# One transformer layer on eight cores: channel-major data, Q beside K and V, and one attention stream that carries the other work as fillers

## What is computed

```python
# 1. half-step SwiGLU FFN (hidden width 2816) on latents and context
x   = x   + 0.5 * g1  * swiglu(modulate(rmsnorm(x)))
ctx = ctx + 0.5 * cg1 * swiglu(modulate(rmsnorm(ctx)))
# 2. token mixer on one normalised input
h, hc = modulate(rmsnorm(x)), modulate(rmsnorm(ctx))
q, k, v, f, ga, gf = split(h @ w_in)     # 8 q heads, 2 kv heads of 128, f: 4 groups of 128
k_c, v_c = split(hc @ w_in[:, kv columns])
q, k = rope(headnorm(q)), rope(headnorm(k));  k_c = headnorm(k_c)
y_attn = softmax(q [k_c, k]^T / sqrt(128)) [v_c, v]            # 2304 keys
y_four = real(fft2(f over (2048 positions, 128 channels)))     # per group, unitary
mix = (sigmoid(ga) * (y_attn @ w_ab) + sigmoid(gf) * (y_four @ w_fb)) @ w_o
x = x + g2 * mix
# 3. second half-step SwiGLU FFN on the latents
x = x + 0.5 * g3 * swiglu(modulate(rmsnorm(x)))
```

## Time and profile before

| what | value |
|---|---|
| median of 3 runs | 2266.95 us |
| span of the profiled execution, slowest core (core 5) | 2253.1 us |
| what the median has above that span | 13.85 us |
| PE busy | 1989.8 us (88%) |
| DVE, ACT, POOL busy | 960.2, 793.6, 322.9 us |
| start, before the first FFN matmul | 0 to 65.9 us |
| first FFN | 65.9 to 690 us |
| K, V, F | 690 to 820 us |
| sequence transform | 820 to 897 us |
| input and Q of tile 0 | 897 to 942.5 us |
| attention, merge and Q, output projection | 942.5 to 1733.5 us |
| last FFN and stores | 1733.5 to 2253.1 us |

### The profile page before, as it was taken

The page is one execution under the profiler, slowest core; times in us unless marked ns, Lnnn a source line. Parts: engine busy times, 40 slices in busy tenths (PEclk is TensorE's granted clock), DMA queues, the critical chain, the costliest instruction groups (busy, mean ns, idle before and its releaser), DMA issues.

```text
span 2253.1 us, 29761 instructions; the slowest of 8 cores (2246.0 to 2253.1 us)
## 1 busy us (share of the span) xinstructions
PE 1989.8 (88%) x9570; PEld 875.1 (39%) x9570; DVE 960.2 (43%) x1310; ACT 793.6 (35%) x1338; POOL 322.9 (14%) x404
## 2 busy tenths in 40 slices
PE   2599998999997777689989998999997999899998
PEld 1244443444443333233433443343332443344344
DVE  0245345343444311554464455444533534533434
ACT  1342110111114630476758557666723310011011
POOL 1341000000004410310320121030014300000000
PEclk9899999999998898799999999999998999999999
DMA  9834244132303443400830380083046132203013
GB/s 176 174 66 75 36 77 66 32 62 38 57 14 63 75 87 101 71 1 1 141 66 1 66 141 1 1 136 66 1 84 103 30 57 38 46 2 56 1 38 112
DMA packets 46084, 138.48 MB, mean 61 GB/s; under 512 B 5104, under 2 KB 5360, under 8 KB 45808
## 3 DMA queue, kind: packets, MB, share of 16 engines
q0 software_dynamic: 31104, 109.07, 29.0%
q1 hardware_dynamic: 12528, 23.34, 3.2%
q10 hardware_dynamic: 2304, 4.20, 0.6%
HBM read 237.24 MB, written 8.39 MB: 109 GB/s over the span
## 4 chain that ended last, share of the span: by engine, by line
PE 74%; DVE 9%; issue 5%; ACT 4%; DMA 3%; POOL 3%; DVEq 0%; ACTq 0%; SPq 0%; POOLq 0%
PE ps L618 14%; PE ps L612 14%; PE ps L640 10%; PE ps L911 9%; DVE xT L645 5%; PE ps L963 5%; PE ps L946 5%; PE ps L964 4%; POOL arena L463 2%; PE ps L1052 2%; PE ps L929 2%; PE ps L444 2%; DMA tmpf<-x 2%; DVE tmpf L1001 1%; PE ps L967 1%
## 5 line engine op out<-in xcount | busy, mean ns | idle before, releaser
L626 ACT ACTIVATE tmpf<-ps 128x512 f32<-128x512 f32 (+1 forms) x198 | 113.4, 573 | 809.5 <-PE ps L612 798.9
L628 DVE TENSOR_TENSOR arena<-ps,tmpf 128x512 bf16<-128x512 f32 (+1 forms) x198 | 130.4, 661 | 494.2 <-PE ps L618 428.8
L645 DVE SCALAR_TENSOR_TENSOR xT<-ps,cols,xT 128x512 f32<-128x512 f32 x384 | 285.4, 750 | 104.4 <-PE ps L640 82.8
L640 PE MATMUL ps<-arena,ring 128*128 128x512 bf16 (+1 forms) x1168 | 278.6, 364 | 28.3 <-DVE xT L645 8.9
L612 PE MATMUL ps<-arena,ring 128*128 128x512 bf16 (+1 forms) x1136 | 258.4, 371 | 10.8 <-POOL arena L463 9.4
L618 PE MATMUL ps<-arena,ring 128*128 128x512 bf16 (+1 forms) x1072 | 242.6, 369 | 0.0
L953 ACT ACTIVATE arena<-ps 128x512 bf16<-128x512 f32 x320 | 185.5, 596 | 109.6 <-PE ps L946 102.0
L463 POOL TENSOR_SCALAR arena<-tmpf,cols 128x512 bf16<-128x512 f32 (+1 forms) x144 | 160.9, 1129 | 214.8 <-DVE tmpf L456 214.8
L911 PE MATMUL ps<-arena,ring 128*128 128x512 bf16 x768 | 171.4, 380 | 5.4 <-DVE arena L1003 5.4
L640 PEld LDWEIGHTS ps<-arena,ring 128*128 128x128 bf16 x1168 | 95.1, 96 | 189.2 <-issue 125.1
L953 ACT ACTIVATE pt<-ps 128x512 bf16<-128x512 f32 x256 | 152.4, 596 | 31.3 <-DVE tmpf L972 15.6
(11 more groups left out here) (115 smaller groups left out, 2214.1 us busy)
## 6 DMA issues: line engine op xcount, KB each, us to landing
ring<-w_in POOLq DMA_DIRECT2D x66, 512.0 KB, 8.3
ring<-w_ffn_in POOLq DMA_DIRECT2D x31, 512.0 KB, 7.2
ring<-w_ada POOLq DMA_DIRECT2D x24, 512.0 KB, 17.3
ring<-w_ffn_out POOLq DMA_DIRECT2D x16, 512.0 KB, 10.1
ring<-w_ab POOLq DMA_DIRECT2D x16, 512.0 KB, 9.4
ring<-w_o POOLq DMA_DIRECT2D x16, 512.0 KB, 9.2
out<-tmpf SPq DMA_DIRECT2D x32, 256.0 KB, 2.0
arena<-w_ffn_in POOLq DMA_DIRECT2D x13, 512.0 KB, 9.5
```

The costliest lines, as they stand in the source:

```text
L626: P.op("act", lambda e, pg=pg, sg=sg: e.activation(out=tmpf[:, sg, 0:n], in_=ps[pg][:, 0:n], func=AF.Silu), reads=[ps_b[pg]], writes=[tmpf ...
L628: P.op("dve", lambda e, pu=pu, sg=sg, jj=jj: e.tensor_tensor(out=act[par][:, jj, 0:n], in0=ps[pu][:, 0:n], in1=tmpf[:, sg, 0:n], op=ALU.mult),
L640: ins = e.matmul(ps[po][:, 0:n], wo3[:, jj % 2, m * 128:(m + 1) * 128], act[par][:, jj, 0:n], start=(jj == 0), stop=(jj == cg - 1))
L645: P.op("dve", lambda e, m=m, po=po: e.scalar_tensor_tensor(out=b["xsl"](m), in0=ps[po][:, 0:n], scalar=cols[:, b["ig"], m:m + 1], in1=b["x ...
```

## The change

The whole program behind the buffers is reordered. What it does, part by part:

- **Data layout.** x, the context and the output are laid out by the host in chunks of channels, so the PE transposes, their copies and the identity go. x is loaded by `load_x` straight into `xT`, block by block in the order latent 0, context, latent 1, 2, 3; the load of a later block waits on SP until PE has reached the block before it. The cosine and sine tables come with the last block. POOL no longer waits for ada tile 7 before it requests FFN weights; SP does before the context load.
- **Start** (`first_block`). The statistics of block 0 and the products with x are made before the ada tiles are consumed. Then the modulation is split: ACT 2 chunks, POOL 1, DVE 5.
- **Normalised input.** Elsewhere the modulation alternates between ACT and POOL.
- **FFN.** The 8 output chunks of a block are spread between the input matmuls of the next block (`carry`, `Spread`), over groups and into the K/V/Q stretch. In the last group the mixer's normalised inputs of blocks 0, context and 1 are side work.
- **K, V, F and Q in one pass** (`p1_run`). Each latent block has 10 heads (2 K, 8 Q) in a pipeline of three stages (`pipe_step`), with V and F units between them. The squares for blocks 2 and 3 are on POOL. The normalised input of each block is stored to HBM, and so is Q of blocks 0 to 2; block 3 is attended first (`ORDER2`). No barriers are left; `inherit` hands the old readers of a region to the new buffers.
- **Sequence transform** (`fourier_thunks`). It folds position n with 2048 - n and frequency m with 2048 - m: 64 half-width channel matmuls as before, then 16 sequence matmuls for each of 4 groups and some small ones. It runs as fillers in attention tile 0. ACT and DVE combine the sums, POOL writes the four quarters.
- **Attention** is one stream of 4 x 8 x 18 = 576 steps without seams, with one filler of two matmuls per step. Of the sums over keys only 3 of 18 stay on PE; 9 exponentials per head are added on DVE (8 adds and a join) and 6 on POOL (5 adds). 8 buffers hold exponentials, before 4.
- **Merge and output** (`merge_thunks`) of a tile are the 144 fillers of the next tile. Sigmoid is computed as (1 + tanh(x/2)) with the factor 0.5 in the column of the output gate. The order of the mid matmuls is ga, gf, fb, ab, in two PSUM banks. The last tile's merge runs alone, with the statistics of the first two blocks of the last FFN.
- **Stores** go from `xT` directly.

```diff
+        def first_block():
+            ...
+            for th in ffn_mh_thunks(blocks, 0)[:12]:
+                th()
+            for m in range(NCH):
+                P.op("dve", lambda e, m=m: e.tensor_tensor(out=xr[m], in0=b["xsl"](m), in1=tmpf[:, 1, :], op=ALU.mult), ...)
+            for t in range(8):
+                ada_consume(t)
+            ...
+        def load_next(bi):
+            if bi < 5:
+                P.wait("sp", [("pe", P.cnt["pe"])])
+                load_x(ORDER1[bi])
...
+                    sp = Spread(side, max(1, 2 * cg - max(1, cg // 2)))
+                    so = Spread(carry, 2 * cg)
+                    def between(sp=sp, so=so):
+                        so.pop()
+                        sp.pop()
+                    for jj in range(cg):
+                        ffn_in_unit(b, pa, jj, between)
...
+            def norm():
+                P.op("pe", lambda e: e.matmul(ps[3][:, 0:n], ones_bf, sq, start=True, stop=True), ...)
+                P.op("act", ... AF.Ln ...)
+                P.op("act", ... AF.Exp, scale=-0.5 ...)
+                P.op("dve", lambda e: e.scalar_tensor_tensor(out=o, in0=ps[pb][:, 0:n], scalar=vecs[:, vgain:vgain + 1], in1=rv, ...))
+            def cosm():
+                P.op("pool", lambda e: e.tensor_tensor(out=qc, in0=qn, in1=cos_bf[...], op=ALU.mult), ...)
+            def rope():
+                P.op("pe", lambda e: e.matmul(ps[6][:, 0:n], rperm_bf, qn, start=True, stop=True), ...)
+                P.op("dve", lambda e: e.tensor_tensor(out=rs, in0=ps[6][:, 0:n], in1=sin_bf[...], op=ALU.mult), ...)
+                P.op("dve", lambda e: e.tensor_tensor(out=dst, in0=qc, in1=rs, op=ALU.add), ...)
...
+            return mh_thunks(..., hb, 7, sqs=sq_pt, ts=(5, 5, 6, 7), sq_eng="pool")
...
+                chunks(6, wget(hga), c0, lambda k: hh[:, k, :], hh_b, 8, lambda sa=sa: late.append(lambda: tanh(6, sa)))
+                chunks(7, wget(hgf), c0, lambda k: hh[:, k, :], hh_b, 8, lambda sf=sf: late.append(lambda: tanh(7, sf)))
+                chunks(6, wget(hfb), c0, lambda k: yfour[:, k, t * 512:(t + 1) * 512], [...], 4, lambda sf=sf: gate(6, sf))
+                chunks(7, wget(hab), c0, lambda k: Y[:, k, :], Y_b, 8, fin_ab)
...
-            DEN_ROLE = "PPPDPPPDPPPDPPPDPP"
+        ROLE = "DDGDDGDDGDGDGDGPPP"
...
+                def join():
+                    P.op("dve", lambda e: e.tensor_tensor(out=acc, in0=acc, in1=accg, op=ALU.add), ...)
+                def den():
+                    P.op("pe", lambda e: e.matmul(ps[5][:, 0:512], ones_f[:], acc, start=False, stop=True), ...)
+                    P.op("dve", lambda e: e.reciprocal(out=rec, in_=ps[5][:, 0:512]), ...)
+                    P.op("dve", lambda e: e.tensor_tensor(out=Q[:, h, :], in0=ps[po][:, 0:512], in1=rec, op=ALU.mult), ...)
+                defer[g + 2] = join
+                defer[g + 4] = den
+        for g in range(len(steps)):
+            if h == 0 and s == 0 and i == 0:
+                fill = fourier_thunks()
+            if h == 0 and s == 0 and i > 0:
+                ...
+                fill = merge_thunks(i - 1)
+            P.op("act", ... out=PT, in_=ps[g % 3][:, 0:512], func=AF.Exp, scale=ATTN_SCALE ...)
+            for f in late:
+                f()
+            del late[:]
+            if g + 2 < len(steps):
+                s_op(g + 2)
+            if fill:
+                f = fill.pop(0)
+                if f is not None:
+                    f()
+            pv_op(g)
+            if g in defer:
+                defer.pop(g)()
+        fill = merge_thunks(3)
```

1434 lines of the change are left out of this document (769 added, 665 removed).

## The result

The changed kernel takes 1990.63 us (median of 5 runs, 1975.17 to 2127.97), against 2435.36 (median of 5, 2265.24 to 2508.79) for the kernel before beside it. Cores at a lowered clock stretch the upper ones of both, so the ratio is that of the least disturbed runs (1975.17 and 1988.09 against 2265.24 and 2266.95): 0.8745, 95% interval 0.8621 to 0.8868. The forecast was 1870, range 1800 to 1965. Direction and most of the gain are right; the time is above the range.

The account below looks back on a forecast made before the run. PE (TensorE), 88% busy, was taken as the bound. Stages 45 + 134 + 437 + 153 + 0 + 610 + 468 = 1847, plus 10 for seams and 14 around the span, gave 1871, stated as 1870; range 1800 to 1965 us.

Parts of the forecast that it names:

- rivals B to E: B: fillers without friction, 1803 us, chance 0.10; D: table loads at each tanh, 1930, 0.04; rival C, Rival E listed separately.
- Start and first group: Start up to the first FFN matmul 45 us; first FFN group 134, with PE idle for early ada tiles until 87.
- No DVE-released PE idle in the FFNs: Sign of being right: spreading outputs between input matmuls ends PE's waits for DVE's residual adds in the FFNs.
- 148 m = 32 us: PE work per latent block in K/V/F/Q; m is one 512-column matmul, 0.216 us at full clock.
- Stream, the step that failed: Attention stream with merges: tile 0 122, tiles 1 to 3 420, last merge 68, together 610 us.
- Interference of DVE and POOL, 2 us per head: Attention: a third to a half of 9 DVE adds per head slowed by POOL, 0.41 to 0.6 us each.
- Rival A: DVE and POOL pace the attention stream: up to 1980 us, with two thirds of it 1945; chance 0.20.
- I add 3.5 for banks that wait while DVE sits in a reciprocal: 140 each.: Attention tiles 1 to 3: PE's 136.5 us per tile plus 3.5 of bank waits gives 140 each.
- Tile 0 ... 15.2 per head on DVE, 122.: Attention tile 0, with the sequence transform: DVE's work of 15.2 us per head sets 122 us; PE has 97.
- rival C: Fillers wait for their banks and don't fill, so merge comes after attention: 148 us a tile, 1895; chance 0.05.
- Rival E: Slower than before: TensorE's clock at 1.2 GHz throughout the stream doubles its 568 us of matmul: 2440; chance 0.02.
- The 14 us between span and median: Whole kernel: median was 13.85 us above the profiled span of 2253.1 before; carried over as 14.

Follow-up runs that it names:

- experiments 8: Changed kernel with other roles in tile 0 alone: more exp tiles summed by ones matmuls on TensorE, fewer adds on DVE and POOL; 1957.89 us, ratio 0.8666.
- 13: Changed kernel with tile 0's transform filler order alone rewritten to 18 steps per group, in phase with the heads; 1952.64 us, ratio 0.8660.
- 15: Changed kernel with both tile 0's in-phase filler order and its new roles; cores 0 to 3 span 1931.9 to 1935.7 us.

## Why the prediction came out as it did, point by point

**Bound, unit, stages.** Right. TensorE at 0.216 us per 512-column matmul is the base, its busy share rose to 91%, and rivals B to E did not come. Every stage was put too short, by 1 to 16%.

**Start and first group** (45 and 134). Right within 7.5 us, but by errors that cancel. The hole before the early ada tiles is there, three waits of some 3.5 us, and it ended at 78, not at 87:

```profile
69.14 0.56 PE L370 MATMUL ps<-csb,ring 128*128 128x2 bf16 x16 [3.43 <-DMA ring<-w_ada]
```

Behind it the group took 108.5 us where my sum has 92, although 32 of its 144 m of outputs ran only later (see K, V, F, Q). What I had not seen is 11.0 us of FFN outputs waiting for residual adds, the longest 5.1, waits of 5.5 for POOL's affines, and a clock of 0.85 over the group.

**FFNs.** 443.6 and 479.0 for 437 and 468. TensorE waits 6.8 us for residual adds in the one; in the other 5.4 for such adds, 4.3 for the first inputs. "No DVE-released PE idle in the FFNs" was wrong, by 11.0 us in the first group and by little behind it.

**K, V, F, Q** (153, measured 168.4). The 153 were 132 of TensorE's work and 21 of waits: 16 for the squares and "5 for the last head's chain". The waits came to 22.2, but that is luck: the squares made 4.1 and the chain 5.5, and 8.0 came at the V matmuls, which take a bank that a residual add still reads (with them in a free bank the stage took 6.2 us less). That bank was in the code to be seen. The step that failed is "148 m = 32 us" per block. The stage's rows add up to 658 m, 142 us. In it are 33 matmuls of FFN outputs, which `carry` moves here from the FFN and which my sum has in the FFN's first group, and the 16 of the statistics of blocks 2 and 3, which it has nowhere; together 10.6 us:

```profile
L573 PE MATMUL ps<-arena,ring 128*128 128x512 bf16 x33 | 8.2, 387 | 0.0
```

**Stream, the step that failed: 610 for 666.** By its terms:
- *Interference of DVE and POOL, 2 us per head.* Right in kind, rather high: 1.3 in the sums, by leaving POOL's out, and 0.2 in the join (mean 897 ns for 690). The Trainium skill, page "SBUF — State Buffer", section "SBUF: two separate sides", has DVE and POOL take a port pair in turn, each for a whole instruction, and says so only of DVE operations with two inputs in SBUF or in a 2-port mode. Rival A added POOL's 6.9 us to the whole of DVE's 12.8, 19.7 a head, and so to the reciprocal, the product and the gates, which read PSUM. That sum did not come: the trace has 17.0 between reciprocals in the freest heads. For the single add, of 1.39 to 1.57 us where POOL works beside it, the trace agrees with the page.
- *"I add 3.5 for banks that wait while DVE sits in a reciprocal: 140 each."* This is the failed term. Above the 136.5 of TensorE's work tile 1 took 11.8 us more and tile 2 14.4 (148.3 and 150.9), so 8 to 11 above the 140. The long wait was not for a bank: it ran through three queues, and came once per tile where the orders of 14 and 18 steps meet. I had counted for each engine how much it works, and for no filler what stands in front of it. With the merge add moved, tiles 1 and 2 took 141.7 and 140.8: without that crossing the 3.5 was nearly right. The Trainium skill, page "PSUM — Partial Sum Buffer", section "Engine vs sequencer instructions", calls the queues of ScalarE, VectorE and GpSimdE strict FIFO; the timeline above agrees, POOL idle for 8.20 us with a ready sum behind.
- *"Tile 0 ... 15.2 per head on DVE, 122."* The busy time was right to a tenth. Four heads of tile 0, mean DVE 15.28 in 18.9 us:

```profile
sum 75.69, PE 57.95 PEld 21.64 DVE 61.13 ACT 41.47 POOL 46.59; mean PE 14.49 PEld 5.41 DVE 15.28 ACT 10.37 POOL 11.65
```

  What failed is to take an engine's busy time for the stage's length. The combination's bank makes TensorE wait for DVE, and then DVE waits for exponentials that TensorE has not fed: 15.3 us of work in a head of 18.9. That the two together make the length is shown by the square of experiments 8, 13 and 15: either remedy alone left 139.4 and 142.4 us, both gave 126.9. Against rival C I wrote that "four steps (3.7 us) lie between free and need": a reciprocal and its product take 4.1.
- *Last merge* (68). 77.8. Waits for tanh make 5.5 of the difference; four table loads of 1283 ns lie there, and nothing is left to work beside them. I did not try to shorten it.
- *"The 33 steps left, 28 us, cover" the loads.* Right, and with little to spare: a transform that ends 16 steps later costs 8.1 us.

**Tanh.** Right: one load at the stream's first tanh, at 941.68, and none after it between exponentials. The two others at the tanh stand in the last merge, each behind a Ln of the next FFN's statistics:

```profile
L434 ACT ACT_TABLE_LOAD x12 | 15.4, 1283 | 18.3 <-PE ps L430 18.3
L557 ACT ACT_TABLE_LOAD x10 | 12.8, 1283 | 0.7 <-PE ps L546 0.5
L1137 ACT ACT_TABLE_LOAD x3 | 3.8, 1283 | 0.6 <-PE ps L1117 0.6
```

**Clock.** Rival E, the low level over the stream, did not come: 0.95 in tile 0 and 0.98 in tiles 1 to 3. Still, my sum has every matmul at full clock; if only the two levels occur there, that costs up to 7 us in tile 0 and 9 in tiles 1 to 3 (an estimate: 0.05 of 141.0 and 0.02 of 447.5), part of the stages' differences above. The other term that I put at nothing is that a part of the cores could lose clock in the dense FFN. That is 29.8 us of the time, on the slowest core.

**The 14 us between span and median.** I carried them over as a fixed cost. In every run of this record whose cores are listed, the time is only 1.5 to 2.8 us above the slowest core's span; in the median run here core 7 spans 1989.1 of 1990.63, at a clock of 0.943. So 1.5 of the 17 us here are fixed, and the rest comes from cores slower in another execution; that the 14 carried over and the 17 come out alike is luck.

Sum: 1871 forecast, 86.8 of stages and seams, 29.8 of clock on core 6, 3 more between span and median: 1990.6. With the clock loss the time left the range; on another chip the same kernel, at 1950.72, lies inside. That does not make the mechanism right: it is above the 1825 to 1930 that the forecast's own terms allowed, and inside only because the range was widened for rival A, which did not come.

## What to carry to other kernels

Count for each engine not only how long it works but what each short instruction stands behind: one long operation (here a reciprocal of 3.36 us) in an in-order queue delays all that follow, and the delay travels through the next engine's queue if something there waits at its head. Where two patterns of different period are interleaved, look for the step at which they meet, or give them the same period; cut the long operation in two if that is cheap. When a remedy moves a wait and not the time, there is a second limit beside the first: try the two together before giving either up.
